# Another row order for the weights of the first expert stage: one 16 KB piece per partition, strided gather and turns

## The reference, cut to what matters

```
def _hier_moe(h, rt_g, rt_g_b, rt_e, rt_e_b, ex_gate, ex_up, ex_down):
    ...
    def expert_block(args):
        idx, w, e = args
        xb = tok_pad[idx]
        hb = jax.nn.silu(xb @ ex_gate[e]) * (xb @ ex_up[e])
        return (hb @ ex_down[e]) * w[:, None]
```

## Time and profile before

| | |
|---|---|
| median of three runs | 2497.46 us |
| the profiled execution's own time | 2494.89 us |
| its span (first to last instruction) | 2493.1 us |
| mean granted TensorE clock | 0.915 of full speed |
| the 16 passes of the first expert stage, from the first L2058 to the end of the last L2079 | 770.34 to 1275.18 us |

### The profile page before, as it was taken

One profiled execution on the slowest core, in us unless ns is written; L12 is line 12 of the kernel. 1 busy time (PEld: TensorE's weight loads), 2 busy tenths in 40 slices (PEclk: granted clock), 3 DMA queues, 4 the chain that ended last, 5 costly groups with the idle time before them and its releaser, 6 DMA issues.

```text
span 2493.1 us, 32555 instructions
## 1 busy us (share of the span) xinstructions
PE 2172.3 (87%) x14114; PEld 1490.3 (60%) x14114; DVE 726.5 (29%) x1525; ACT 455.3 (18%) x932; POOL 12.7 (1%) x20
## 2 busy tenths in 40 slices
PE   6999883338699999999989999999989899999998
PEld 4454662337674444444447568886867778847844
DVE  1285247573632111111123420001653330000001
ACT  2210123212121111111122421001331320000001
POOL 0000000000000000000000000000000000000000
PEclk8999966658899999999999999999988789999999
DMA  9352000000348999999974573423540119799796
GB/s 320 130 198 101 1 1 0 1 1 2 123 155 319 393 394 394 394 394 394 394 286 171 182 252 129 172 93 128 210 170 1 62 68 349 258 374 360 258 342 242
DMA packets 231400, 511.99 MB, mean 205 GB/s; under 512 B 8926, under 2 KB 32173, under 8 KB 230893
## 3 DMA queue, kind: packets, MB, share of 16 engines
q1 hardware_dynamic: 230512, 509.87, 55.6%
q10 hardware_dynamic: 765, 0.31, 0.0%
HBM read 509.11 MB, written 1.05 MB: 205 GB/s over the span
## 4 chain that ended last, share of the span: by engine, by line
PE 69%; DMA 14%; DVE 10%; ACT 3%; SPq 3%; issue 1%; POOL 0%; ACTq 0%; DVEq 0%; POOLq 0%
PE PS L377 32%; DMA work<-in_ex_up_dram 10%; PE PS L2058 6%; PE PS L2212 4%; PE PS L1915 3%; DMA work<-in_moe_w_gate_up_dram 2%; PE PS L568 2%; PE PS L2163 2%; SPq L1835 2%; PE PS L1979 1%; PE PS L1990 1%; PE PS L576 1%; PE PS L671 1%; DMA work<-in_w_ada_dram 1%; PE PS L2079 1%
## 5 line engine op out<-in xcount | busy, mean ns | idle before, releaser
L377 PE MATMUL PS<-hT,work 128*128 128x256 f32 x1456 | 327.7, 386 | 0.4 <-ACT hT L737 0.4
L377 PEld LDWEIGHTS PS<-hT,work 128*128 128x128 f32 x1456 | 279.4, 193 | 43.1 <-issue 2.8
L377 PE MATMUL PS<-work 128*128 128x256 f32 (+4 forms) x960 | 285.5, 458 | 9.9 <-DVE work L1664 5.8
L2058 PE MATMUL PS<-work,sq 128*64 128x512 f32 x1024 | 233.9, 611 | 25.5 <-DMA work<-in_ex_up_dram 24.2
L377 PEld LDWEIGHTS PS<-work 128*128 128x128 f32 (+2 forms) x960 | 178.6, 187 | 112.7 <-issue 76.5
L2058 PEld LDWEIGHTS PS<-work,sq 128*64 128x64 f32 x1024 | 82.8, 140 | 173.3 <-issue 173.3
L377 PE MATMUL PS<-sq,work 128*128 128x128 f32 x1408 | 160.2, 277 | 8.1 <-DMA work<-in_moe_w_gate_up_dram 8.1
L377 PEld LDWEIGHTS PS<-sq,work 128*128 128x128 f32 x1408 | 159.9, 194 | 10.0 <-issue 10.0
L2079 PE MATMUL PS<-work 128*64 128x512 f32 x512 | 113.4, 595 | 9.8 <-issue 9.8
L2212 PE MATMUL PS<-work 128*64 128x512 f32 (+1 forms) x352 | 114.4, 593 | 1.9 <-ACT work L2242 1.9
L1979 PEld LDWEIGHTS PS<-work,xc 128*128 128x128 f32 x768 | 87.9, 192 | 14.0 <-issue 13.9
(11 more groups left out here) (549 smaller groups left out, 2260.1 us busy)
## 6 DMA issues: line engine op xcount, KB each, us to landing
work<-in_ex_gate_dram SPq DMA_DIRECT2D x32, 2048.0 KB, 17.7
work<-in_ex_up_dram SPq DMA_DIRECT2D x32, 2048.0 KB, 19.2
work<-in_ex_down_dram SPq DMA_DIRECT2D x32, 2048.0 KB, 14.2
work<-in_moe_w_gate_up_dram SPq DMA_DIRECT2D x32, 2048.0 KB, 10.4
work<-in_ada_w_dram SPq DMA_DIRECT2D x24, 2048.0 KB, 8.5
work<-in_moe_w_down_dram SPq DMA_DIRECT2D x16, 2048.0 KB, 15.5
work<-in_w_ada_dram SPq DMA_DIRECT2D x12, 2048.0 KB, 8.8
work<-in_moe_w_gate_up_dram SPq DMA_DIRECT2D x16, 1536.0 KB, 13.1
```

Of the source, the lines that this page charges most:

```text
L377: ins = pe.matmul(outp, lhs, rhs, start=n == 0, stop=n == len(pairs) - 1, **kw)
L2058: ins = pe.matmul(PS[pair[m], 6 + j, :], xs[:, k, pair[m]], unit(U[name] + 3 * m + j, KT, F)[:, k, :], start=k == 0, stop=k == KT - 1)
```

## The change

In `moe1` partition p now takes the rows that follow each other: of a gate or up matrix rows 8 p to 8 p + 7, of a down matrix rows 4 p to 4 p + 3. In HBM that is one run of 16 KB per partition, and it also lies in one run in the slot. So that the other operand agrees, step k of the gather takes feature columns k, k + 8, k + 16, ... (32 bytes apart), and turn f takes hidden columns f, f + 4, f + 8, ... (16 bytes apart). The same instructions are issued in the same order with the same waits. The branch that is taken when an expert has too many tokens gets 16 more transposes and two more copies; it does not run here.

```diff
+        if name == "moe1":
+            return w.rearrange("(p k) n -> p k n", p=P)
         if what == "down":
             return w[t0 * P:(t0 + n) * P, :].rearrange("(k p) n -> p k n", p=P)
         return ktiles(w, c0 + t0 * P, n * P)
+
+    def ptile(name, t, n):
+
+        return slice(t, n * P, n) if name == "moe1" else slice(t * P, (t + 1) * P)
...
-                ins = pe.matmul(PS[:, 4 + k // 4, (k % 4) * P:(k % 4 + 1) * P], htok[:, tt, k * P:(k + 1) * P],
+                ins = pe.matmul(PS[:, 4 + k // 4, (k % 4) * P:(k % 4 + 1) * P], htok[:, tt, ptile(name, k, KT)],
                                 pickG[:, tt, :], start=tt == 0, stop=tt == 1)
...
-                ins = pe.transpose(PS[:, 6, f * P:(f + 1) * P], htk[:, f * P:(f + 1) * P], ident)
+                ins = pe.transpose(PS[:, 6, f * P:(f + 1) * P], htk[:, ptile(name, f, FT)], ident)
...
+        n_rows = 2 * COUNT[name] // 4
+        if name == "moe1":
+            for tt in range(2):
+                for k in range(KT):
+                    ins = pe.transpose(PS[:, 2 * tt + k // 4, (k % 4) * P:(k % 4 + 1) * P], htok[:, tt, ptile(name, k, KT)], ident)
+            ins.then_inc(S["rowsum_" + name], 1)
+            n_rows += 1
+        pe.wait_ge(S["rows_" + name], n_rows)
```

More of the change, by code:

```diff
@@ L1891, in ex_pe @@
                                 ins = product(PS[:, 4 + (g - g0) % 4, j * N:(j + 1) * N],
-                                              [(w[:, k, t * P:(t + 1) * P], hT[:, k, :]) for k in range(KT)], paced=paced)
+                                              [(w[:, k, ptile(name, t, n)], hT[:, k, :]) for k in range(KT)], paced=paced)
                                 if j == 0 and owed:
@@ L2313, in weight_rows_pe @@
                 .then_inc(S["rowsum_" + name], 1)
-        pe.wait_ge(S["rows_" + name], 2 * COUNT[name] // 4)
+        n_rows = 2 * COUNT[name] // 4
[6 more added lines that the diff above has]
+        pe.wait_ge(S["rows_" + name], n_rows)
     def weight_rows_act(name):
@@ L2321, in weight_rows_act @@
                            PS[:, 6 + r % 2, :].rearrange("p (e t) -> p e t", t=P), ACT.Copy).then_inc(S["rows_" + name], 1)
+        if name == "moe1":
+            act.wait_ge(S["rowsum_" + name], 2 * COUNT[name] // 4 + 1)
+            for tt in range(2):
+                ins = act.activation(hT[:, :, tt * P:(tt + 1) * P],
+                                     PS[:, 2 * tt:2 * tt + 2, :].rearrange("p b (k n) -> p (b k) n", n=P), ACT.Copy)
+            ins.then_inc(S["rows_" + name], 1)
     def weight_rows_dve(name):
```

## The result

The changed kernel took 2529.23 us, the median of four runs between 2521.82 and 2533.79 us. The kernel before, on the same chip, took 2495.74 us (four runs, 2491.16 to 2501.66). The ratio is 1.013 with a 95% interval of 1.0094 to 1.0166, so the change costs 33.5 us. The forecast was 2526 us. The profiled execution took 2533.79 us, its span is 2532.0 us, and its mean granted clock is 0.918 (0.915 before).

A forecast was written before the change was run, and what follows sets the result against it. DMA's up-matrix loads bound 13 of 16 passes; after the change TensorE would. Stage: 3.6 (first gather) + 16 x 33.26 = 535.8 against 504.8 us, so +31 on 2494.9 gives 2526 us, own range 2512 to 2538.

The forecast's parts named there:

- The bound: First expert stage: DMA's up-matrix landing holds up 13 of 16 passes; faster loading can return at most 35.8 us.
- Both paces: Time per pass of the expert stage before the change: 29.31 us for TensorE, 31.93 us for DMA.
- The loads: Expert weights in 16 KB pieces: 420 GB/s taken (410 to 430), 29.96 us a pass, hidden whole under TensorE.
- the faster rival: Strided gather loads and turns keep the present pace, DMA sets 29.96 us a pass; -25 us, 2470 us; chance 0.12.
- The gather: Its 32 stationary loads, columns 32 bytes apart, take 225 instead of 111.6 ns: +3.6 us per gather, 17 gathers.
- The turns: Four strided loads ahead of the down products: +0.35 us on the path, bounds 0 and +0.46, 16 times.
- even: Gather loads cost 150 to 190 ns, or turns and part of the gather hide; around 2495 us; chance 0.04.
- Loads and products one after the other: In the gather, 225 ns loads no longer run beside products: +6.9 us a pass, +89 us, 2584 us; chance 0.04.
- The slower HBM: Partitions read exactly 16 KB apart slow the weight loads to 345 GB/s: 36.5 us a pass, 2574 us; chance 0.04.
- What was to be seen: Profile after: gather about 7.2 us, turns about 0.95, passes about 33.3, no L2058 wait for up, full queue over 410 GB/s.

The follow-up runs named there:

- the last experiment: The kernel of the first experiment, with down matrices again in 4 KB pieces and turns side by side; 2463.72 us, ratio 0.9877.
- the first experiment: Changed kernel, but ScalarE's copy from PSUM puts the tokens in the new order once, so gathers read neighbouring columns; 2458.96 us, ratio 0.9858.
- the third: Changed kernel with gate and up in 8 KB or 4 KB pieces and gather columns 16 or 8 bytes apart; 2526.5 and 2474.64 us.
- step 2: Changed kernel with gate and up in four 4 KB pieces and gather columns 8 bytes apart; 2474.64 us, ratio 0.9922.
- step-4 kernel: Changed kernel with gate and up in two 8 KB pieces and gather columns 16 bytes apart; 2526.5 us, ratio 1.014.
- cut-in-two kernels: Gather products cut into two of 64 tokens, in the changed kernel (2693.17 us) and in that of the first experiment (2534.93 us).
- s8_strides_only: Changed kernel with gather and turns strided but weights loaded as before, so operands don't match; 3072.52 us, ratio 1.2323, second block took another branch.
- half_side_by_side: The kernel of the first experiment with each gather product cut into two of 64 tokens; 2534.93 us, ratio 1.016.
- the test made for it: Changed kernel with each strided gather product cut into two of 64 tokens, so twice as many loads; 2693.17 us, ratio 1.0794.

## Why the prediction was right

**The bound.** Both paces were as read. TensorE's own pass of 29.31 us appears bare in the last experiment, and 29.35 us in the first. DMA's excess of 35.8 us was the most that faster loading could return; the first experiment returned 35.0 us of it in the stage (504.8 - 469.8). The waits of the earlier trace rows are only 24.2 us of it. Most of the rest is TensorE at the low clock right behind them: five times the half of L2058 that follows the landing takes 8.80 instead of 7.10 us, 8.5 us together, and between 995.0 and 1000.0 us the granted clock is 0.66. DMA still set the pace: from the fourth on the passes start 31.9 us apart on average, which is 12.58 MB at 394 GB/s. In the first experiment the clock stays at 1.00 through the stage.

```profile
963.42 7.10 PE PS L2058 x32
...
1059.20 8.80 PE PS L2058 x32
```

**The loads.** From two piece sizes the fixed part of 10 ns and 74.9 ns per 2 KB gave 430 GB/s for 16 KB, and the changed kernel moves 431. The mixed pieces of the third and the last experiment bear the two rates out: 8.39 MB at 410 and 4.19 MB at 431 GB/s would give 417, and step 2 moves 416; the other way round it would give 424, and the last experiment moves 422. The prediction called 430 the upper end and took 420; the fit was right and the caution was not needed. It changes nothing in the sum, since these loads are hidden, but it changes what the faster rival would have been: at 431 GB/s a pass of loads takes 12.58 MB / 431 = 29.2 us, under TensorE's 29.31, so that rival ends at its own floor, near 2459 us and not at 2470. The first experiment measured 2458.96.

**The gather.** This is the step that decided. Its mechanism held: the load runs beside the product and becomes the longer of the two. Its size was short: 225 ns a load against 238, +3.6 us against +4.06. The price came from lines with 32 and 64 columns, 128 and 256 bytes apart, at 1.76 ns a column, and for 128 columns 16 and 32 bytes apart it is 1.82 and 1.86. Why a column costs a little more here is open; no run varied the number of columns. That distance hardly matters once columns are 16 bytes apart, which the prediction argued from two distances only, holds for four: 16, 32, 128 and 256 bytes (the last two with 32 and 64 columns only).

**The turns.** +0.35 us was taken and +0.04 measured, nearly nine times too much. The rule "a column apart costs 1.76 ns whatever is done with it" failed: their load alone took 141 ns and takes 202, and in the packed trace the last three started 109 ns apart and now start 109 and 118 ns apart, not 225. A turn's load was faster to begin with, so it most likely has more room beside its product; why it is faster was not tested. The lower bound of 0 was the right end, and the earlier trace rows, on which the sentence stood, already said that this load differs from the gather's.

The two errors offset each other: the gathers were 7.8 us too cheap over 17, the turns 5.0 us too dear over 16. A pass is 29.31 + 4.06 + 0.04 = 33.41 us, where the prediction had 33.26. That 2526 and 2529 us lie so close is in part luck. The forecast starts from the profiled execution of before and adds 31 us; the profiled executions lie 38.9 us apart and the medians 33.5, and the four runs of the changed kernel alone spread over 12 us. The profiled spans differ by 38.9 us: 31.6 in the 16 passes, 4.1 in the first gather, 2.4 ahead of it and 0.9 behind the stage, the last two in work that is the same. The prediction had 27.4 us for the 16 passes and 3.6 for the first gather. Of the 31.6 us, 1.4 are the first L2064 at a clock of 0.91 (15.34 us instead of 13.95):

```profile
776.80:792.14 15.34, 15.34 (x65) 5.39 (x65) 0.18 (x1) 2.09 (x9) 0.00 (x0) 0.91 0.38 138
```

The step-4 kernel and both cut-in-two kernels show that too (15.4 to 16.5 us), the other four do not (13.95). It doesn't go with the strides, since s8_strides_only is among the four and half_side_by_side is not; its cause was not tested.

**What the Trainium skill said.** In "SBUF — State Buffer", section "Door 1: The DMA port swizzle", the rule that two hits on a 16-byte line are needed for full speed is what the distances show: 118 ns at 8 bytes, 233 at 16. The page's other sentence, float32 free up to a step of 4, does not hold for the gather, which costs 3.9 us at exactly that step; for the turns at the same step it comes out within 0.04 us a pass. The rule of "TensorE: Matmul & The Clock Gate", section "LDWEIGHTS (loading the stationary operand)", that a load depends on the column count alone, was the faster rival; 112 against 238 ns for the same 128 columns refutes it.

**The rivals.** Faster and even fell with 238 ns a load; a gain needed under 180. At 8 bytes (118 ns) that world exists: 2474.64 us. Loads and products one after the other fell, in the changed kernel (4.06 and not 6.9) and in the test made for it. The slower HBM fell with 431 GB/s. What was to be seen came as written: about 7.2 us for the gather (7.71), 300 ns a record (334), no wait for the up matrix, about 378 GB/s on average (377), over 410 with a full queue (431). Only the turns' 0.95 us was 0.65.

## What to carry to other kernels

When a layout is changed to make a DMA faster, price what it does to the other operand by the engine that becomes the bound: here 17 gathers at +4.06 us are 69 us, against a gain of 36. Put the reordering where it happens once and another engine does it (the copy out of PSUM took the same 1.88 us), not in the stationary load that is repeated for every pair; where a stride must be kept there, keep two float32 columns per 16 bytes. Here a stationary load was free only as long as it was no longer than the product beside it, so look at the load's row by itself, not only at PE.

## What the runs showed that had not been expected

- The jump is between 8 and 16 bytes: 112, 118, 233 and 238 ns for 128 float32 columns at steps of 1, 2, 4 and 8.
- The pace of strided loads is the same at a granted clock of 1.00 and 0.50 (236 to 242 ns).
- The clock fell to 0.50, TensorE's lower level of 1.2 GHz, inside every gather of strided loads beside products of 64 columns, although the records show PE and PEld without a gap (the ends of products are modelled). The same 64 loads side by side kept 1.00 in the pass shown, and so did 32 strided loads beside products of 128 columns. Whether the short products or the length of the stretch (15.3 us) bring it about was not tested.
- One core took 431 GB/s from HBM with 16 KB pieces, and SyncE's issue of two 2 MB loads became ten times shorter (9.26 to 0.81 us). The number of pieces matters there without a queue that is always full: 4.7 to 6.4 us with 2 KB pieces at the changed kernel's pace.
- ScalarE reads PSUM with a step of 8 at the speed of a plain copy (1.88 us for 128x2048).
